# Eight weight pieces a token tile at both ends of the two-tile projections

## What is computed

```python
x = x + gt[:, None] * (y @ w_out[l])                 # first block, last layer: "out1"
# second block, layer 0
h = rms_norm_2(x, norm_pre[0])
proj = h @ a_w_in                                    # "gin": 1024 -> 6144
uv, z = gelu(proj[..., :4096]), proj[..., 4096:]
u, v = uv[..., :2048], layer_norm(uv[..., 2048:], ln_g, ln_b)
y = u * (w_masked @ v + b_s) * silu(z)
x = x + rms_norm_2(y @ a_w_out, norm_post[0])        # "gout": 2048 -> 1024
# second block, layer 1
h = rms_norm_2(x, norm_pre[1])
proj = h @ b_w_in                                    # "din": 1024 -> 10240
x = x + rms_norm_2(dilated_attention(proj) @ b_w_out, norm_post[1])   # "dout"
```

## Time and profile before

| | us |
|---|---|
| runs | 1215.78, 1218.68, 2229.26; median 1218.68 |
| profiled execution | 1212.87 |
| its span | 1211.1 |
| PE busy in the span | 1117.5 (92%) |
| DVE, ACT, POOL busy | 722.9, 601.8, 254.6 |

### The profile page before, as it was taken

The page is one execution under the profiler, slowest core; times in us unless marked ns, Lnnn a source line. Parts: engine busy times, 40 slices in busy tenths (PEclk is TensorE's granted clock), DMA queues, the critical chain, the costliest instruction groups (busy, mean ns, idle before and its releaser), DMA issues.

```text
span 1211.1 us, 16719 instructions
## 1 busy us (share of the span) xinstructions
PE 1117.5 (92%) x5877; PEld 891.8 (74%) x5877; DVE 722.9 (60%) x1320; ACT 601.8 (50%) x1180; POOL 254.6 (21%) x324
## 2 busy tenths in 40 slices
PE   5989999999889879999997999999699999999997
PEld 1667677767668667787775877888588888888785
DVE  3487877777754664753446666663665646455543
ACT  3345454445752446654655544454444455445552
POOL 1582522180005150311202031000122202011100
PEclk8999999999999999999999999999899999999999
DMA  8856464334013233232105846555365664444301
GB/s 331 163 174 199 126 165 122 105 93 151 19 52 109 70 104 88 70 88 70 70 2 166 283 148 199 152 174 187 103 207 176 190 191 125 122 138 123 105 1 52
DMA packets 79290, 157.94 MB, mean 130 GB/s; under 512 B 5792, under 2 KB 6088, under 8 KB 78952
## 3 DMA queue, kind: packets, MB, share of 16 engines
q1 hardware_dynamic: 75880, 147.41, 39.1%
q0 software_dynamic: 3328, 9.46, 3.4%
HBM read 153.73 MB, written 3.11 MB: 130 GB/s over the span
## 4 chain that ended last, share of the span: by engine, by line
PE 74%; DVE 10%; ACT 6%; issue 4%; POOL 3%; DMA 2%; SPq 0%; ACTq 0%; POOLq 0%; DVEq 0%
PE bank L771 17%; PE bank L773 17%; PE bank L772 17%; PE bank L920 5%; PE bank L895 3%; PE bank L905 3%; PE bank L996 3%; DVE w_lo L1726 2%; PE bank L969 2%; POOL small L1536 2%; PE bank L981 2%; PE bank L791 2%; DVE work L1746 2%; ACT w_hi L1123 2%; DMA work<-in_w_ada_dram 1%
## 5 line engine op out<-in xcount | busy, mean ns | idle before, releaser
L771 PE MATMUL bank<-w_lo,h_hi 128*128 128x512 f32 (+1 forms) x1152 | 456.6, 396 | 29.2 <-DVE h_lo L1795 12.6
L773 PE MATMUL bank<-w_hi,h_hi 128*128 128x512 f32 (+1 forms) x1152 | 442.4, 384 | 0.0
L772 PE MATMUL bank<-w_hi,h_lo 128*128 128x512 f32 (+1 forms) x1152 | 441.7, 383 | 0.0
L1726 DVE TENSOR_TENSOR w_lo<-raw,w_hi 128x1024 fp32r<-128x1024 f32 x224 | 287.4, 1289 | 168.8 <-ACT w_hi L1123 167.0
L1123 ACT ACTIVATE w_hi<-raw 128x1024 fp32r<-128x1024 f32 x224 | 235.8, 1058 | 266.7 <-PE bank L773 216.4
L771 PEld LDWEIGHTS bank<-w_lo,h_hi 128*128 128x128 f32 x1152 | 219.0, 190 | 78.7 <-issue 31.0
L773 PEld LDWEIGHTS bank<-w_hi,h_hi 128*128 128x128 f32 x1152 | 218.2, 189 | 43.8
L772 PEld LDWEIGHTS bank<-w_hi,h_lo 128*128 128x128 f32 x1152 | 219.2, 190 | 38.2
L920 PE MATMUL bank<-work,stage 128*128 128x128 f32 x640 | 92.3, 285 | 0.0
L1714 POOL TENSOR_TENSOR stage<-stage 128x512 f32<-128x512 f32 x24 | 41.4, 1742 | 218.3 <-DVE stage L551 218.3
L920 PEld LDWEIGHTS bank<-work,stage 128*128 128x128 f32 x640 | 83.3, 200 | 1.2 <-issue 0.4
(11 more groups left out here) (175 smaller groups left out, 1117.1 us busy)
## 6 DMA issues: line engine op xcount, KB each, us to landing
raw<-in_b_w_in_dram SPq DMA_DIRECT2D x80, 512.0 KB, 3.7
raw<-in_w_in_dram SPq DMA_DIRECT2D x56, 512.0 KB, 4.0
raw<-in_a_w_in_dram SPq DMA_DIRECT2D x48, 512.0 KB, 3.9
raw<-in_w_ada_dram SPq DMA_DIRECT2D x32, 512.0 KB, 3.8
work<-in_w_ada_dram SPq DMA_DIRECT2D x16, 512.0 KB, 11.4
raw<-in_w_out_dram SPq DMA_DIRECT2D x16, 512.0 KB, 3.5
raw<-in_a_w_out_dram SPq DMA_DIRECT2D x16, 512.0 KB, 3.5
raw<-in_b_w_out_dram SPq DMA_DIRECT2D x8, 512.0 KB, 3.5
```

What stands on the lines that cost most here:

```text
L771: pe.matmul(bank, hT(h_hi, ph, at, tt), w_lo[:, s, k, lo:lo + w], start=first, stop=False)
L772: pe.matmul(bank, hT(h_lo, ph, at, tt), w_hi[:, s, k, lo:lo + w], start=False, stop=False)
L773: mm = pe.matmul(bank, hT(h_hi, ph, at, tt), w_hi[:, s, k, lo:lo + w], start=False, stop=last)
L1726: dve.tensor_tensor(w_lo[:, i % SPLIT, :, :], raw[:, PIECE_AT[p] % RAW, :, :], w_hi[:, i % SPLIT, :, :].bitcast(F32), ALU.subtract).then_i ...
```

## The change

Twelve pieces get places of their own in `work` (`EXTRA_BLOCKS`): the four of gin's chunk 0, the last four of gout's chunk 1 and the four of din's chunk 0. The others share the ring as before (`RING`), so eight pieces in a row are split at the same time. With them

- chunks 0 and 1 of gin and din are made together: eight pieces for tile 0, then eight for tile 1;
- the ending of gout is all of chunk 1: eight pieces for tile 0, then eight for tile 1; the endings of out0, out1 and dout keep four;
- tile 0's transposes stand before the sixth of the eight pieces in gout's tile 1 (before the fourth of four in out1, as before); tile 1's before the fifth piece of tile 0 in gin and the sixth in din;
- `end_of` has new orders for two tiles, ACT's and DVE's;
- din's heads of chunk 0 are turned in chunk 2, piece 0.

```diff
-    if ph == "din" or c > 2:
-        return (c - 1, TURNED_AFTER[(n, k)]) if c and (n, k) in TURNED_AFTER else None
+    if ph == "din":
+        if c == 2 and n == 0:
+            return 0, k
+        return (c - 1, TURNED_AFTER[(n, k)]) if c > 1 and (n, k) in TURNED_AFTER else None
...
+EXTRA_BLOCKS = {
+    ("gin", 0, 0): (4096, 5120, 6144, 7168, 14336, 15360, 16640, 17664),
+    ("gout", 1, 4): (0, 1024, 2048, 3072, 16384, 17408, 18432, 19456),
+    ("din", 0, 0): tuple(range(4096, 12288, 1024)),
+}
+EXTRA = {(ph, c, pair + i): at[2 * i:2 * i + 2] for (ph, c, pair), at in EXTRA_BLOCKS.items() for i in range(4)}
+RING = [p for p in SPLITS if p not in EXTRA]
+RING_AT = {p: n for n, p in enumerate(RING)}
+WIDE = ("gin", "din")
+SECOND_TURNED = {"gin": ("gin", 1, 0), "din": ("din", 1, 1)}
+ENDING = {"out0": 4, "out1": 4, "gout": 8, "dout": 4}
...
+        def w_slot(p):
+            if p in EXTRA:
+                return tuple(work_r[:, at:at + 2 * NC].rearrange("p (k n) -> p k n", k=2) for at in EXTRA[p])
+            s = RING_AT[p] % SPLIT
+            return w_hi[:, s, :, :], w_lo[:, s, :, :]
...   # PE, project
+                    if ph in WIDE and c == 0:
+                        for tt in tts:
+                            for p in pieces_of(ph)[:8]:
+                                if tt == 0:
+                                    if p == SECOND_TURNED[ph]:
+                                        norm_turns(ph, 1)
+                                    weights(p)
+                                for k in range(2):
+                                    product(ph, p[1], p, k, tt)
+                    if ph in WIDE and c < 2:
+                        if between:
+                            between(c)
+                        continue
...
-                    ending = pieces[-SPLIT:] if ph in FOLLOWING and c == PROJ[ph][0] - 1 else []
+                    ending = pieces[-ENDING[ph]:] if ph in FOLLOWING and c == PROJ[ph][0] - 1 else []
...
-                            if tt == tts[-1] and p == ending[-1] and FOLLOWING[ph]:
+                            if tt == tts[-1] and p == ending[5 if ph == "gout" else 3] and FOLLOWING[ph]:
...   # ACT, split_until
-                    if i >= SPLIT:
-                        act.wait_ge(*used_last(SPLITS[i - SPLIT]))
+                    if p in RING_AT and RING_AT[p] >= SPLIT:
+                        act.wait_ge(*used_last(RING[RING_AT[p] - SPLIT]))
...   # ACT, end_of
+                if len(tts) == 2:
+                    split_until(first)
+                    process_tile(0)
+                    if ph == "gout":
+                        split_until(first + 2)
+                    squares_of(0)
+                    split_until(first + (2 if ph == "out1" else 5))
+                    norm_tile(following, 0)
+                    split_until(first + (4 if ph == "out1" else 6))
+                    process_tile(1)
+                    split_until(first + (4 if ph == "out1" else 7))
+                    squares_of(1)
+                    split_until(first + 8)
+                    norm_tile(following, 1)
+                    return
...   # DVE, end_of
+                if len(tts) == 2:
+                    split_until(first)
+                    process_tile(ph, 1, 0)
+                    split_until(first + (1 if ph == "out1" else 2))
+                    normalise(following, 0)
+                    split_until(first + (2 if ph == "out1" else 3))
+                    norm_tile(following, 0)
+                    split_until(first + (2 if ph == "out1" else 6))
+                    process_tile(ph, 1, 1)
+                    split_until(first + (4 if ph == "out1" else 7))
+                    normalise(following, 1)
+                    split_until(first + 8)
+                    norm_tile(following, 1)
+                    return
```

More of the change, by code:

```diff
@@ L67, in turned_at @@
 def turned_at(ph, c, n, k):
-    if ph == "din" or c > 2:
-        return (c - 1, TURNED_AFTER[(n, k)]) if c and (n, k) in TURNED_AFTER else None
+    if ph == "din":
+        if c == 2 and n == 0:
+            return 0, k
+        return (c - 1, TURNED_AFTER[(n, k)]) if c > 1 and (n, k) in TURNED_AFTER else None
+    if c > 2:
+        return (c - 1, TURNED_AFTER[(n, k)]) if (n, k) in TURNED_AFTER else None
     tt = FIRST_TURNED.get((c, n, k))
@@ L283, in first_then_second_block @@
         h_lo = sb("h_lo", [P, 4096], F32R)
+        with nc.sbuf_tensor("work_r", [P, WORK_W], F32R) as work_r:
+            pass
         work = sb("work", [P, WORK_W])
@@ L758, in product @@
                 kt = p[2] * 2 + k
-                s = SPLIT_AT[p] % SPLIT
+                high, low = w_slot(p)
                 if kt == 0:
@@ L770, in product @@
                 at = k_tile(ph, c, kt)
-                pe.matmul(bank, hT(h_hi, ph, at, tt), w_lo[:, s, k, lo:lo + w], start=first, stop=False)
-                pe.matmul(bank, hT(h_lo, ph, at, tt), w_hi[:, s, k, lo:lo + w], start=False, stop=False)
-                mm = pe.matmul(bank, hT(h_hi, ph, at, tt), w_hi[:, s, k, lo:lo + w], start=False, stop=last)
+                pe.matmul(bank, hT(h_hi, ph, at, tt), low[:, k, lo:lo + w], start=first, stop=False)
+                pe.matmul(bank, hT(h_lo, ph, at, tt), high[:, k, lo:lo + w], start=False, stop=False)
+                mm = pe.matmul(bank, hT(h_hi, ph, at, tt), high[:, k, lo:lo + w], start=False, stop=last)
                 if last:
@@ L1120, in split_until @@
                     act.wait_ge(*landed[PIECE_AT[p] % RAW].seen(p))
-                    if i >= SPLIT:
-                        act.wait_ge(*used_last(SPLITS[i - SPLIT]))
-                    act.activation(w_hi[:, i % SPLIT, :, :], raw[:, PIECE_AT[p] % RAW, :, :], ACT.Copy) \
+                    if p in RING_AT and RING_AT[p] >= SPLIT:
+                        act.wait_ge(*used_last(RING[RING_AT[p] - SPLIT]))
+                    act.activation(w_slot(p)[0], raw[:, PIECE_AT[p] % RAW, :, :], ACT.Copy) \
                         .then_inc(*weights_hi.at(p))
@@ L1157, in end_of @@
                 following, tts = FOLLOWING[ph], tiles_of(ph)
+                first = SPLIT_AT[(following, 0, 0)]
+                if len(tts) == 2:
[13 more added lines that the diff above has]
+                    return
                 for tt in tts[:-1]:
@@ L1160, in end_of @@
                     squares_of(tt)
-                first = SPLIT_AT[(following, 0, 0)]
-                if len(tts) == 4:
-                    norm_tile(following, 0)
+                norm_tile(following, 0)
                 split_until(first + SPLIT - 1)
-                if len(tts) == 2:
-                    norm_tile(following, 0)
                 process_tile(tts[-1])
@@ L1262, in project @@
                         p = (ph, c, n)
-                        if ph in FOLLOWING and c == PROJ[ph][0] - 1 and n >= pairs - SPLIT:
+                        if ph in FOLLOWING and c == PROJ[ph][0] - 1 and n >= pairs - ENDING[ph]:
                             continue
@@ L1725, in split_until @@
                     dve.wait_ge(*weights_hi.seen(p))
-                    dve.tensor_tensor(w_lo[:, i % SPLIT, :, :], raw[:, PIECE_AT[p] % RAW, :, :],
-                                      w_hi[:, i % SPLIT, :, :].bitcast(F32), ALU.subtract).then_inc(*weights_lo.at(p))
+                    high, low = w_slot(p)
+                    dve.tensor_tensor(low, raw[:, PIECE_AT[p] % RAW, :, :], high.bitcast(F32), ALU.subtract).then_inc(*weights_lo.at(p))
                 at[0] = max(at[0], n)
@@ L1805, in end_of @@
                         normalise(following, tt - 1)
[L1806 to L1809, removed]
+                norm_tile(following, 0)
                 split_until(first + SPLIT - 1)
-                if len(tts) == 2:
-                    norm_tile(following, 0)
                 process_tile(ph, 1, tts[-1])
                 split_until(first + SPLIT)
-                if len(tts) == 2:
-                    normalise(following, 1)
                 for tt in tiles_of(following)[1:]:
```

## The result

Five executions of the changed kernel took 1220.01 to 1227.27 us, median 1224.93; five of the kernel before had the median 1218.68. The ratio is 1.0058 with a 95% interval of 1.0038 to 1.0078; the one execution of the kernel before that took 2229 us is in no ratio. The profiled execution of the changed kernel took 1223.99 us with a span of 1222.3, against 1212.87 and 1211.1 before. The forecast was 1216, 1207 to 1223.

The account below looks back on a forecast made before the run. PE, busy 1117.5 of the 1211.1 us span, was taken as the bound. The profiled 1212.87 + 1.6 (out1 into gin) − 0.45 (gout into din) gave 1214.0; about 2 added for run differences: 1216, range 1207 to 1223.

Parts of the forecast that it names:

- the sum: Whole kernel: 1212.87 + 1.6 (out1 into gin) − 0.45 (gout into din) = 1214.0 us, before adding about 2.
- With 4.3, 5.1 and 6 us to landing: Gin's tile 0: pieces 5 to 7, loaded beside POOL's loads, are late; PE idles 1.7, 0.6 and 1.4 us.
- The bounds: Out1 into gin: by the landings, −0.7 us (all 3.5) to +5.6 us (all near POOL's 9.4).
- rival 3: POOL's loads hold gin's pieces 5 to 7; tile 1 starts 4 us later than forecast: 1220 us. Chance 0.1.
- clock term: Din: half rate behind the 3.35 us idle at tile 1's transposes costs up to 1.6 us; 0.8 taken.
- both `norm_tile(1)` stand behind piece 7: 1.15 more: Gin: tile 1's norm scaling comes behind the split of piece 7, adding 1.15 us to PE's idle.
- the forecast's +1.6: Out1 into gin: idle terms sum to 9.05 us against 7.45 before, so 1.6 us slower.
- The bank wait: Din's chunk 2, second tile, waits for the PSUM bank freed by the rope product of chunk 1, tile 0: +1.75 us.
- The second stall: Din's first product: ACT's splits that wait for DMA delay `norm_tile`; 3.2 us idle, where it was 2.16.
- −0.45 us: Gout into din: −3.0 from the new order, +1.75 waiting for a PSUM bank, +0.8 for the clock.
- rival 2: Both stretches: the cover works, only 5.8 of 17.2 us stay idle: −11.4 us, 1204; halfway, 1210. Chance 0.2.

Follow-up runs that it names:

- Six banks: Changed kernel with late loads, plus six instead of four PSUM banks for din's chunks 0 to 2: 1214.99 us, 0.9980 to the kernel before.
- late loads: Changed kernel with POOL's six loads held until the high part of gin's eighth piece is made: 1215.77 us, 0.9994 to the kernel before.
- three splits instead of five: Changed kernel with late loads, plus three splits instead of five before `norm_tile(0)` on ACT at gout's end: 1215.56 us, 0.9992.
- din part alone: Kernel before with only the gout into din part of the change; out1 and gin as before: 1216.82 us, 1.0003.
- three edits: Changed kernel with POOL's loads behind gin's eighth piece, six banks for din's chunks 0 to 2, three splits before `norm_tile(0)`: 1211.15 us, 0.9944.
- gin part alone: Kernel before with only the out1 into gin part of the change; gout and din as before: 1225.07 us, 1.0070.
- three edits with the loads put back: The kernel with three edits, but POOL's six loads at their old place: 1219.39 us, 1.0014 to the kernel before.
- both controls: Kernel before with POOL's loads held until gin's chunk 1, piece 0: all six, 1225.57 us, 1.0085; all but the spatial weights' load, 1218.27 us, 1.0020.
- the two edits: Six banks for din's chunks 0 to 2 and three splits before `norm_tile(0)`; added to the din part alone: 1212.32 us, 0.9965.
- two of six loads: Changed kernel with two of POOL's loads (1.5 MB) ahead of gin's eighth piece and four behind it: 1222.06 us, 1.0054.

## Why the prediction was wrong

The measured time lies 2 us above the range. In the pair of profiles the sum had +1.15 us, and +11.1 was measured: 10 us more. Some 3.2 of them are the clock in unedited stages. Gin cost 8.2 us more than forecast, and there it is one term and the clock behind it; gout into din did 1.4 us better.

**The step that failed**: "With 4.3, 5.1 and 6 us to landing: ready 665.2, 667.2, 670.0, idle 1.7, 0.6, 1.4." Measured: the sixth and seventh piece landed in 3.6 and 5.3 us, idle 0.7 and 1.2; the eighth in 11.8, idle 7.5. The prediction had the moment of issue about right (behind 661.65, with POOL's loads from 659.3; it was 662.7 and 660.67) and the landing wrong: 2.0 us into the burst, 2.5 of the 3.8 MB were ahead of the piece. The bounds came from pieces of the order before, and no such piece was issued in the middle of the burst: one at 661.41, 1.3 us into it, landed in 5.1 us, and the next, at 669.8 and later, in 6.5 at most. The row of a 1 MB load that took 9.4 us stood beside them; it was made into rival 3, "no piece took over 6.5 us beside these loads", at 0.1. The mechanism of rival 3 is what happened; its price (+4, 1220) was too low, since it took 9.4 us for the landing and left out the clock.

**The clock in gin.** The 7.5 us of idle were followed by half rate: 13 intervals of 0.43 instead of 0.23 us, 2.6 us more. The forecast had a clock term only in din. On the other hand "both `norm_tile(1)` stand behind piece 7: 1.15 more" cost nothing, since the slow matmuls covered it. Sum for gin: 6.1 + 2.6 − 1.15 over the forecast's +1.6 is 9.1; measured +9.8.

**What held in gin.** Transposes forecast for 651.6, came at 651.69; tile 0 forecast for 655.45, came at 655.97 (behind a slow spell of the clock); tile 1's transposes without a wait (661.83), as forecast.

**gout into din.** Most steps held. T0 is the end of gout's chunk 0, set 0.2 us ahead of its split as in the prediction (829.0; 840.33 after), and T1 the end of tile 0 (853.5 after); the times with a plus are counted from T1:

| step | forecast | measured |
|---|---|---|
| T0 to T1 | 13.05 | 13.15 |
| PE waits ahead of the first transposes | 1.4 | 1.9 |
| ACT begins `norm_tile(0)`, behind splits that wait for DMA | +13.6 | +12.9 |
| din's first product | +16.3, after 3.2 of idle | +15.5, without a wait |
| tile 1's transposes | +26.45, after 3.35 of idle | +25.6, after 3.1 |
| the wait for the rope product | 1.75 | 1.6 |
| chunk 2's second tile starts, from T0 | 57.8 | 57.1 |

The bank wait stood in no wait of the kernel before and was found from the order alone. Six banks took it away, in part as forecast. The second stall did not come as forecast: no wait where 3.2 us stood, because the three pieces ahead of din's first product ran mostly at half rate (the granted clock was 0.66 from 865 to 868) and took 5.8 us instead of 4.08, and ACT was 0.7 us early. With late loads, where that stretch was at full rate, the wait was 1.5 us, and three splits instead of five took it away: the splits that wait for DMA did hold the norm, for half of the time forecast. The clock term (0.8, up to 1.6) stood behind tile 1's transposes. Half rate came there in three other profiles with this part (the din part alone, six banks, the three edits) and not in this one. Up to the attention this part brought 1.8 us, where −0.45 us was forecast with the clock and −1.25 without. That the whole from T0 on came out near the forecast is luck: the slow spell in the attention, which the forecast did not have, took the gain back.

**The cover** (rival 2) did not work as a whole: waits for `normalise` in din fell only from 5.9 to 5.0 us, since the splits are in line on ACT and DVE, as the prediction argued; the separate measurement of this part (1.0003, interval from 0.9989) leaves out the 0.995 that a full cover would give.

## What to carry over

Ask of every load that an edit makes urgent which other queue's bulk it is issued into, and bound its landing by the length of that whole burst, not by the landings of loads that met its edges. Eight pieces a tile instead of four double the cover, but also halve the time between two loads that are needed: in gin, with three raw places, what was left after the loads were moved (1.5 and 0.9 us of waits for weights) came from the reload. Bulk loads that are wanted late belong behind the last urgent one, and a late load has to be checked for its own first user.

## What the runs showed of the hardware

**A load behind another queue's burst.** A 512 KB load from SP took 4.4 us to landing with none of POOL's loads ahead, 8.5 with 1.5 MB and 11.8 with 2.5 MB ahead, at 394 GB/s on the DMA engines in all. At the same place in the burst, 2.0 us behind its first load, it took 12.0 us with the gin part alone and 11.2 in the three edits with the loads put back. In these traces loads landed nearly in the order of issue across the two queues; the clear exceptions were issued within 0.3 us of each other: before, the piece at 661.41 landed at 666.5, ahead of a 1 MB load issued at 661.12 (669.0); with the late loads one issued at 666.8, only 0.8 us into the burst, landed behind the 1 MB load issued 0.2 us after it, and took 10.6 us.

The Trainium skill, "DMA: Bandwidth & Descriptors" (Queues, rings and completion order), says that each DMA engine takes turns between the queues it has work for, packet by packet. SP's queue and POOL's from 655 to 690 (packets, MB, share of 16 engines):

```profile
q1 hardware_dynamic: 1860, 3.58, 29.9%
q0 software_dynamic: 736, 3.80, 28.8%
```

POOL's packets are 2.7 times as long, so by such turns, as an estimate, SP would get 27% of the 394 GB/s: 4.9 us of transfer for a piece instead of 1.3, and a landing near 8 us. The 8.5 us with 1.5 MB would fit that, 11.8, 12.0 and 11.2 don't; the order of landing and the growth with the bytes ahead are nearer to waiting for the bytes issued before. Why is not shown.

**The clock after a wait.** Half rate (a granted clock of 0.50) followed the idle of 7.5 and 4.6 us. After shorter waits it came or not, at the same place in the program (the profiles by their experiment; "late loads" is the first):

| idle of PE | half rate followed | full rate followed |
|---|---|---|
| 3.4 us, gin's first product | both controls, din part alone with and without the two edits | before |
| 3.0 to 3.1 us, din's tile 1 | din part alone, six banks, three edits | after, late loads |
| 2.5 us, layer norm | after, two of six loads, din part alone | before, late loads, gin part alone |
| 2.0 us, gin's tile 0 | after, six banks, two of six loads, three edits | late loads |
| 1.5 us, attention | all five with din's new order and four banks | the nine others |

An idle stretch of 1.5 to 3.4 us is thus a risk and no certain cost. It makes single profiles of one kernel differ by more than the effect of a small edit. Whole executions show it too: of 29 of the kernel before on one chip, the fastest took 1211.38 us at a mean granted clock of 0.983 and the slowest 1219.77 at 0.973.
